# One-core PEER decoder step: one-hots, gather rows, V products and the residual issued in another order around the U and V sweeps

## The reference, cut to what matters

```python
def _layer(x, ...):
    h = _rmsnorm(x, norm1_g)
    ...
    merged = jax.nn.sigmoid(zga) * a_out + jax.nn.sigmoid(zgb) * b_out
    x = x + merged @ w_mix_out
    x = x + _peer(_rmsnorm(x, norm2_g), peer_wq, peer_k1, peer_k2, peer_u, peer_v)

def _peer(...):           # e: expert indices (tokens, 128), g: their softmax weights
    act = jax.nn.gelu(jnp.einsum('tkd,td->tk', u_tab[eb], hb))
    return jnp.einsum('tk,tkd->td', gb * act, v_tab[eb])

y_prompt = _rmsnorm(xp, final_g)
```

## Time and profile before

| | us |
|---|---|
| median of 3 runs (4887.19 to 4899.76) | 4889.77 |
| profiled execution, its time | 4888.54 |
| its span, first to last instruction | 4886.8 |
| PE busy | 4675.6 |
| DVE busy | 2655.6 |

### The profile page before, as it was taken

The page is one execution under the profiler, slowest core; times in us unless marked ns, Lnnn a source line. Parts: engine busy times, 40 slices in busy tenths (PEclk is TensorE's granted clock), DMA queues, the critical chain, the costliest instruction groups (busy, mean ns, idle before and its releaser), DMA issues.

```text
span 4886.8 us, 47196 instructions
## 1 busy us (share of the span) xinstructions
PE 4675.6 (96%) x18798; PEld 3394.6 (69%) x18798; DVE 2655.6 (54%) x4623; ACT 535.2 (11%) x1220; POOL 892.9 (18%) x691
## 2 busy tenths in 40 slices
PE   8999999999999999899999999999999989999995
PEld 7888888888756566566667678888888734444442
DVE  3433300018658576635555467775777755545555
ACT  1111200001111101110000111111222200000000
POOL 1000000000111212003333231112333222222222
PEclk9999999999999999999999999999999999999997
DMA  4334334553776758548889788778899899999997
GB/s 162 145 137 144 143 144 167 193 188 123 242 269 221 296 204 315 200 168 354 346 340 358 273 334 317 269 279 293 329 335 333 312 393 414 413 373 417 417 417 292
DMA packets 237853, 1352.17 MB, mean 277 GB/s; under 512 B 43185, under 2 KB 43441, under 8 KB 131138
## 3 DMA queue, kind: packets, MB, share of 16 engines
q1 hardware_dynamic: 143778, 665.97, 37.0%
q0 software_dynamic: 93856, 683.19, 36.0%
HBM read 1308.38 MB, written 40.16 MB: 276 GB/s over the span
## 4 chain that ended last, share of the span: by engine, by line
PE 56%; DMA 23%; DVE 14%; issue 4%; ACT 1%; POOL 1%; POOLq 0%; SPq 0%; DVEq 0%; ACTq 0%
PE ps L357 30%; PE ps L632 11%; DMA RING<-in_peer_v,table 7%; DMA RING<-in_peer_u,table 7%; PE ps L553 5%; DVE CUR L836 4%; DMA RING<-in_peer_v,X 4%; DVE RING L830 4%; DMA RING<-in_peer_u,X 4%; PE ps L495 3%; DVE BIG L1102 2%; PE ps L559 1%; PE ps L373 1%; DMA out<-BIG 1%; PE pm L402 1%
## 5 line engine op out<-in xcount | busy, mean ns | idle before, releaser
L357 PE MATMUL ps<-X,BIG 128*128 128x320 f32 (+1 forms) x5632 | 1400.1, 410 | 7.1 <-DVE BIG L1200 6.5
L357 PEld LDWEIGHTS ps<-X,BIG 128*128 128x128 f32 x5632 | 1070.8, 191 | 320.1 <-issue 18.1
L836 DVE SCALAR_TENSOR_TENSOR CUR<-RING,wexp,CUR 128x2048 f32<-128x2048 f32 x320 | 752.1, 2350 | 397.5 <-DMA RING<-in_peer_v,table 292.4
L830 DVE CUSTOM_DVE_ANT_0 RING<-RING,CUR 128x2048 f32<-128x2048 f32 x320 | 729.7, 2289 | 413.9 <-DMA RING<-in_peer_u,table 278.5
L632 PE MATMUL ps<-X,RA 128*128 128x256 f32 x4096 | 902.9, 381 | 5.4 <-DMA RA<-in_uT 4.0
L632 PEld LDWEIGHTS ps<-X,RA 128*128 128x128 f32 x4096 | 777.3, 191 | 112.2 <-DMA RA<-in_uT 4.3
L1800 POOL DMA_INDIRECT RING<-in_peer_u,table x256 | 364.9, 1426 | 1335.4 <-DVE hidden L830 991.5
L1800 POOL DMA_INDIRECT RING<-in_peer_v,table x256 | 363.0, 1418 | 1132.9 <-DVE CUR L836 814.4
L655 PE MATMUL ps<-RA,BIG 128*128 128x512 f32 x1024 | 489.7, 601 | 23.0 <-DMA RA<-in_peer_v 14.8
L655 PE MATMUL pm<-RA,BIG 128*128 128x512 f32 x1024 | 481.6, 592 | 0.0
L655 PEld LDWEIGHTS ps<-RA,BIG 128*128 128x128 f32 x1024 | 191.5, 191 | 279.4 <-issue 200.7
(11 more groups left out here) (291 smaller groups left out, 2923.8 us busy)
## 6 DMA issues: line engine op xcount, KB each, us to landing
BIG<-in_w_in_b SPq DMA_DIRECT2D x64, 2048.0 KB, 8.9
RA<-in_uT SPq DMA_DIRECT2D x256, 512.0 KB, 5.5
RA<-in_peer_v SPq DMA_DIRECT2D x256, 512.0 KB, 9.4
BIG<-in_w_gb_b SPq DMA_DIRECT2D x16, 2048.0 KB, 8.4
BIG<-in_w_ga_b SPq DMA_DIRECT2D x16, 2048.0 KB, 8.2
BIG<-in_w_gla_o_b SPq DMA_DIRECT2D x16, 2048.0 KB, 10.1
BIG<-in_w_mix_b SPq DMA_DIRECT2D x16, 2048.0 KB, 9.8
BIG<-in_w_q_b SPq DMA_DIRECT2D x16, 2048.0 KB, 9.3
```

Of the source, the lines that this page charges most:

```text
L357: last = pe.matmul(bank[:, 0:n], w[:, k, j * P:(j + 1) * P], src[:, k, 0:n], start=(k == 0), stop=(k == kt - 1))
L830: row_used.on(dve.tensor_tensor_reduce(out=row, in0=row, in1=h2cur[0:n, :], scale=1.0, scalar=0.0, op0=ALU.mult, op1=ALU.add, accum_out=hi ...
L836: row_used.on(dve.scalar_tensor_tensor(out=cur[0:n, :], in0=row, scalar=wexp[0:n, par, k:k + 1], in1=cur[0:n, :], op0=ALU.mult, op1=ALU.ad ...
```

## The change

- `G_AT` becomes 63, so the last gate product comes in U block 126 and block 127 has none. In a gated block DVE now runs `gate_tokens` of the block before, then the argument, then the one-hots of the next block, then H, and the rows last (budget 4.5 instead of 4.2). Before block 62 the budgets are 3.9 for routing and 2.8 for rows (3.6 and 2.0 before).
- Rows at more places: one at each of three points of `new_sample_states` in each head of group 1, budgets 14.4 and 9.6 in the first step of `gates(1)`.
- The change of tile: the gain is loaded into `h2cur` as soon as the last U row of a tile is used; the sum of squares goes to the ring; U rows of the next tile wait only for `query_in` (the load of `h2cur`), V rows for `cur_loaded`. The gather of the third row of a tile waits for the squares of the tile before.
- V by tile at its ends: block 0 multiplies tile 1 (in `pm`) for both halves ahead of tile 0, and the last two blocks do all of tile 0 ahead of tile 1.
- The residual comes back in 8 pieces of 256 KB and the gain in 4, one behind every eighth load of V from load 48 on.
- The end runs by tile, with squares in 4 pieces, the output in halves.

```diff
-G_AT = NB - PT // 4
+G_AT = NB - PT // 4 - 1
...
             pe.wait_ge(*gm_ready.at(PT // 4 - 1))
-            for b in range(NB):
+            for half in range(2):
+                v_product(0, half, 1)
+            pe.wait_ge(*h_ready.at(NB - 1))
+            for half in range(2):
+                v_half.on(v_product(0, half, 0), 0, half)
+            for b in range(1, NB - 2):
                 for half in range(2):
...
+                    v_product(b, half, 0)
+                    v_half.on(v_product(b, half, 1), b, half)
+            for t in range(2):
+                for b in range(NB - 2, NB):
+                    for half in range(2):
+                        last = v_product(b, half, t)
+                ps_done.on(last, "tile", t)
...
                     if b:
                         sample_state(h, b - 1)
+                    if b in (2, 4, 6):
+                        run(work, 2.4)
...
             def gates(g):
+                if g:
+                    spare((0, "gates1"), 14.4)
                 center(g)
                 finish(g, HEADS - 1)
+                if g:
+                    spare((0, "gates2"), 9.6)
                 layer_norm(g)
...
                 bank = banks.of("u", b)
+                if b > G_AT:
+                    gate_tokens(b - 1 - G_AT, b)
                 dve.wait_ge(*sq_u.at(b))
...
-                if b > G_AT:
-                    gate_tokens(b - 1 - G_AT, b)
                 spare((b, "u"), 0.0)
-                if b < G_AT:
-                    paced(work_1, 3.6)
-                paced(work, 2.0 if b < G_AT else 4.2)
+                if b < G_AT - 1:
+                    paced(work_1, 3.9)
+                    paced(work, 2.8)
+                elif b < NB - 2:
+                    onehots(b + 1 - G_AT)
...
-                if G_AT - 1 <= b < NB - 1:
-                    onehots(b + 1 - G_AT)
-            gate_tokens(PT // 4 - 1, NB)
+                if b >= G_AT - 1:
+                    paced(work, 4.5)
...
             def cur_load(t):
...
+                query_in.dma(pool.dma_start(h2cur[0:n, :], h2_d[t, 0:n, :]), t)
+                if t:
+                    yg_stored.dma(pool.dma_start(o[0][0, (t - 1) * P:t * P, :], cur[:, :]), t - 1)
+                    pool.wait_ge(*yg_stored.at(t - 1))
...
+            def gain_load(t):
+                pool.wait_ge(*row_used.at(last_u[t]))
+                fg_cur.dma(pool.dma_start(h2cur, a["final_g"].rearrange("(o d) -> o d", o=1).partition_broadcast(P)), t)
...
+                if m % ROWS == 2 and t:
+                    pool.wait_ge(*ss_g.at(t - 1))
...
-                if m == 2 * NB + 24:
-                    for t in range(2):
-                        x2_back.dma(sp.dma_start(x2b[:, t, :], x2_d[2 + t]), *((t,) if t == 0 else ()))
...
+                i = (m - 2 * NB - 48) // 8
+                cols = slice(512 * (i % 4), 512 * (i % 4) + 512)
+                if (m - 2 * NB) % 8 == 0 and 0 <= i < 8:
+                    x2_back.dma(sp.dma_start(x2b[:, i // 4, cols], x2_d[2 + i // 4, :, cols]), *((i,) if i < 7 else ()))
+                elif (m - 2 * NB) % 8 == 0 and 8 <= i < 12:
+                    fg_loaded.dma(sp.dma_start(final_g[:, cols], a["final_g"].rearrange("(o d) -> o d", o=1)[
+                        :, cols].partition_broadcast(P)), *((i,) if i < 11 else ()))
```

More of the change, by code:

```diff
@@ L645, in _, with v_product @@
                     ps_done.on(last, "g", q)
-            pe.wait_ge(*gm_ready.at(PT // 4 - 1))
-            for b in range(NB):
-                for half in range(2):
-                    m = 2 * NB + 2 * b + half
-                    pe.wait_ge(uv_loaded[slot_of[m]].sem, loads_of[m])
-                    for t in range(2):
[L653 to L657, removed]
+            def v_product(b, half, t):
+                m = 2 * NB + 2 * b + half
+                pe.wait_ge(uv_loaded[slot_of[m]].sem, loads_of[m])
+                for q in range(2):
+                    last = pe.matmul((ps, pm)[t][:, 2 * half + q, :], H[:, b, t * P:(t + 1) * P],
+                                     vhalf[slot_of[m]][:, q * 512:(q + 1) * 512], start=(b == 0), stop=(b == NB - 1))
+                return last
+            pe.wait_ge(*gm_ready.at(PT // 4 - 1))
+            for half in range(2):
[4 more added lines that the diff above has]
+            for b in range(1, NB - 2):
+                for half in range(2):
+                    v_product(b, half, 0)
[5 more added lines that the diff above has]
+                ps_done.on(last, "tile", t)
         @block.vector
@@ L853, in gather_rows @@
                             dve.wait_ge(*halves_met.at())
-                            step(dve.tensor_tensor(cur[0:NS, :], cur[0:NS, :], h2cur[0:NS, :], ALU.add))
-                        step(dve.tensor_tensor_reduce(out=h2cur[0:n, :], in0=cur[0:n, :], in1=cur[0:n, :], scale=1.0,
+                            step(dve.tensor_tensor(cur[0:NS, :], cur[0:NS, :], ring[0:NS, (m - 3) % 3, :], ALU.add))
+                        step(dve.tensor_tensor_reduce(out=ring[0:n, (m - 1) % 3, :], in0=cur[0:n, :],
+                                                      in1=cur[0:n, :], scale=1.0,
                                                       scalar=0.0, op0=ALU.mult, op1=ALU.add,
@@ L1297, in gate_tokens @@
                 dve.wait_ge(*ps_done.at("g", q))
[L1298 to L1299 removed]
+                dve.wait_ge(*g_copied.at(q))
                 dve.wait_ge(*h_ready.at(n - 1))
@@ L1349, in _ @@
                                  t, q)
-            for t in range(2):
-                dve.wait_ge(*ss3_done.at(t))
-                ms3_ready.on(dve.tensor_scalar(small[:, 14 + t:15 + t], small[:, 12 + t:13 + t], 1.0 / D, EPS, ALU.mult,
+                dve.wait_ge(*ss3_done.at(t, 3))
+                step(dve.tensor_reduce(small[:, 20 + t:21 + t], small[:, 12 + 4 * t:16 + 4 * t], AX.X, ALU.add))
+                ms3_ready.on(dve.tensor_scalar(small[:, 20 + t:21 + t], small[:, 20 + t:21 + t], 1.0 / D, EPS, ALU.mult,
                                                ALU.add), t)
-            dve.wait_ge(*fg_loaded.at())
-            for t in range(2):
                 dve.wait_ge(*root3.at(t))
-                step(dve.reciprocal(small[:, 16 + t:17 + t], small[:, 14 + t:15 + t]))
-                y_ready.on(dve.scalar_tensor_tensor(out=x2b[:, t, :], in0=x2b[:, t, :], scalar=small[:, 16 + t:17 + t],
-                                                    in1=final_g, op0=ALU.mult, op1=ALU.mult), t)
+                step(dve.reciprocal(small[:, 22 + t:23 + t], small[:, 20 + t:21 + t]))
+                for half in range(2):
+                    cols = slice(1024 * half, 1024 * half + 1024)
+                    y_ready.on(dve.scalar_tensor_tensor(out=x2b[:, t, cols], in0=x2b[:, t, cols],
+                                                        scalar=small[:, 22 + t:23 + t], in1=final_g[:, cols],
+                                                        op0=ALU.mult, op1=ALU.mult), t, half)
         @block.scalar
@@ L1716, in _ @@
                 serve(("end", i))
-            act.wait_ge(*fg_loaded.at())
+            act.wait_ge(*v_half.at(NB - 3, 1))
             for t in range(2):
[L1719 to L1723, removed]
+                for q in range(4):
+                    cols = slice(512 * q, 512 * q + 512)
+                    act.wait_ge(*sum_ready.at(t, q))
+                    ss3_done.on(fn(junk[:, t, cols], x2b[:, t, cols], ACT.Square,
+                                   accum_out=small[:, 12 + 4 * t + q:13 + 4 * t + q]), t, q)
                 act.wait_ge(*ms3_ready.at(t))
-                root3.on(fn(small[:, 14 + t:15 + t], small[:, 14 + t:15 + t], ACT.Sqrt), t)
+                root3.on(fn(small[:, 20 + t:21 + t], small[:, 20 + t:21 + t], ACT.Sqrt), t)
         @block.gpsimd
@@ L1802, in gather @@
                     bass.IndirectOffsetOnAxis(ap=idx, axis=0), bounds_check=NEXP - 1, oob_is_err=True), m)
+            last_u = [TOPK * max(i for i, unit in enumerate(units) if unit[0] == t and unit[2] == "u") + TOPK - 1
+                      for t in range(3)]
             cur_load(0)
```

63 lines of the change are left out of this document (32 added, 31 removed).

## The result

| | before | after |
|---|---|---|
| median, us | 4897.22 (4879.05 to 4914.12, 20 runs) | 4869.08 (4853.22 to 4884.82, 20 runs) |
| profiled execution, its time | 4888.54 | 4884.4 |
| its span | 4886.8 | 4882.7 |

The ratio is 0.9943, with a 95% interval of 0.9931 to 0.9956. The change gives 0.6% where 1.9% was forecast, and the time lies above the whole range (4764 to 4830). So the two profiles show 4.1 us between them where the medians show 28.1. I account for the span of the profiled execution first, and say at the end where its excess lies.

A forecast was written before the change was run, and what follows sets the result against it. The gather chain ended last, 27 us behind PE, the bound beneath. PE's end 4826.2+4+1+0-30-4.7-13.5 = 4783.0, plus 11.5 gave a span of 4794.5 and, with 1.74 and 1.2 added, 4797 us; 80% range 4764 to 4830.

The forecast's parts named there:

- Part 5: More rows in the sample section, gates(1) and ungated U blocks: +4 (0 to +24), +1 (0 to +6), 0 (-2 to +10) us.
- Part 4: V sweep, 906.1 us before: cut residual and gain loads shorten PE's waits, -13.5 us, bounds -20 and +5.
- a slack of 0.8 us: V sweep: fitted with 200 GB/s to the two old waits, subtracted from each piece's 1.3 us, leaving 0.5.
- Rival D: Residual and gain pieces in the V sweep pay a fixed cost each, +18 us: 4815; chance 0.07.
- The stall on load 4 of V: V sweep: allowance for load 4 arriving late, taking the sum from -15.3 to -13.5 us.
- Part 2: Gated U blocks: PE's wait for one-hots goes, 8.67 to 8.2 us a block, -30 us (bounds -54 and -1).
- My slot cycle: Gated U blocks: the second row waits for the slot the block before used first; 8.2 us a block on average.
- a sign of being wrong: Forecast is wrong if gated blocks take over 8.7 us, or if PE waits for U loads.
- rivals C and F: Gated U blocks. C: new wait replaces the old, 4826 us, chance 0.2. F: U loads bind, 4936 us, chance 0.03.
- Part 3: U to V: the 9.2 us between u(127) and V falls to 4.5, -4.7 us (0 to -8).
- Part 1: V sweep: 180 rows left instead of 226; the gather ends some 145 us ahead of PE and leaves the end.
- Part 6: The end: 11.5 us (9.5 to 14) from PE's last matmul to the end of the span.

The follow-up runs named there:

- The run with DVE's time alone: Changed kernel with an unused DVE reduction of a row's length replacing the row at three points of new_sample_states, so no gather starts: 4832.9 us, ratio 0.988.

## Why the prediction was wrong

- **Part 5, the sample sections: the step that failed.** I had +4 with bounds 0 and +24; it is +57 in the profiled execution. In the six profiled kernels that share all code up to the U sweep, the first U product starts at 2966.5, 2961.0, 2956.8, 2954.2, 2950.9 and 2948.8, so +47 is typical. The kernel before and the one with one-hots first, which share theirs, have 2909.3 and 2920.1, so that some 42 us are left between the two means, as by the medians (41.6). Of the 15.3 us by which the profiled execution exceeds its median, some 10 lie here, and 5 in its U sweep (986.3 us, where the eight profiled kernels with this code there have 981.5 on average). I named the right chain (store, then load, then PE), and priced it by DVE's 2.3 us. The run with DVE's time alone shows that this costs nothing. The price is that of a gather of 1 MB set off by the row, which lengthens each store and load of the chain, and, on top, PE's lower clock behind each wait. I had put 2 us of clock behind each V wait, and none here; the 12 us that I expected for in_state_gla are 30.4. My own question, what a faster engine triggers and what that collides with, would have led here: the earlier trace rows show room on DVE, and say nothing of SP's chain. Gates(1) at +1 is within what was seen.
- **Part 4, V sweep: wrong in sign (+13.9 for -13.5).** The step is "a piece of 256 KB costs 1.3 - 0.8 = 0.5 us". The first two waits behind pieces come 30.2 us apart in after, where eight loads take PE 27.5:

```profile
4135.65 1.98 PE L651 MATMUL ps<-RA,BIG 128*128 128x512 f32 x4 [0.82 <-DMA RA<-in_peer_v]
...
4165.81 1.98 PE L651 MATMUL ps<-RA,BIG 128*128 128x512 f32 x4 [1.68 <-DMA RA<-in_peer_v]
```

  That is 2.7 us for this piece. Over all twelve waits, the last at 4458.30, it is (4458.30 - 4135.65) / 11 = 29.3 us, so 1.8 us a piece, and the run that moves them gives 25 us for the twelve (920 - 895), 2.1 each, where I had 0.5. I had taken a slack of 0.8 us off each piece. My reading is that under the gather the V loads do not win it back between pieces, so that it can be spent once; no run shows that by itself. Without it my term would have been 12 x 1.3 = 16 us. Rival D pointed there, with a chance of 0.07, and would still have had the sweep at +4.5. The Trainium skill, "DMA: Bandwidth & Descriptors", section "Anatomy of one DMA", gives a fixed 2.0 us to each DMA on the path that POOL issues on (the pieces are SP's); the profiles have 1.3 for each further one, so less, yet far from my zero. The stall on load 4 of V came at 3975.04, but with 5.53 us and a slow group of 3.78 behind it, where I had allowed 1.8 in all and had said that no V wait would pass 2 us. These 5 to 6 us and the 21 that the pieces cost beyond my 4 are the miss of 27.4.
- **Part 2, gated blocks: the old wait rightly named, the new one not (8.41 for 8.2).** The wait for the one-hots is gone. By budgets 0, 3.6, 4.2 and 4.5 the blocks take 7.81, 7.90, 8.14 and 8.41 us; the seven other profiles at 4.5 have 8.25 to 8.42, and the mean of the eight is 8.35. My slot cycle, (7 x 8.6 + 5.4) / 8, gives 8.2 for the last; for 4.2 it gives (6 x 8.6 + 2 x 5.4) / 8 = 7.8. It runs 0.15 to 0.35 us low, and that it comes so near is in part luck. DVE does wait longer for rows, as I said it would, but PE never waits for DVE or ACT in these blocks. From 3410 to 3940 us it waits for U loads alone:

```profile
PE ps L632 <- DMA RA<-in_uT: 27.4, 25, 2.5
```

  That is 27.4 of the (8.41 - 7.81) x 63 = 38 us by which these blocks exceed PE's pace, and it is what I had named as a sign of being wrong: the transfer side of rivals C and F at a small size. The DMAs carry 353 GB/s here instead of 329:

```profile
3410.00:3940.00 530.00, 502.53 (x2526) 440.48 (x2525) 437.97 (x636) 143.66 (x446) 169.40 (x117) 0.99 0.93 353
```

  The gated part gives -17 us instead of -30. The ungated blocks gave about 6 us that I had not counted, and block 127, which now has no gate product and stands behind the last one, takes back 2.5.
- **Part 3, U to V: right.** 4.1 us for 4.5.
- **Part 1, fewer rows in V: right.** The gather leaves the end, and its last row is 167 us ahead of PE for the 145 I had. Three more rows (183) and a change of tile of 18.8 us instead of 13 made it later, not earlier; the margin is wider because V itself took 27 us longer than forecast. The gather had in fact more room than was needed, and that room was where the sample rows belonged: worked off in V they cost nothing that shows (V sweep 919 us against 920).
- **Part 6, the end: right.** 9.9 us for 11.5.

No rival had the loss in the heads, so the range (4764 to 4830) had no case for it. The parts that I had worked out from a stall in view (1, 3, 6, and the direction of 2) held. The two that failed were additions: the cover of the rows I had judged by DVE when SP's chain was the one at risk, and that of the pieces by a slack seen behind single large loads. Their bounds rested on these two readings, and so they were too narrow.

## What to carry to other kernels

An instruction that frees a buffer can cost what the transfer behind it does to the chains of small transfers around it, not its own time: look for a store that a load waits for and that PE waits for, and keep large gathers out of it. A short wait of PE is to be priced with the lower clock that follows. Once the gather no longer ends last, every row and every piece belongs where only spare DMA time is used. A slack found behind one large load is better not counted again for each piece.

## What the runs showed of the hardware that I had not expected

- Behind waits of only 4.44 and 2.74 us in a section whose groups are small, groups of four took 3.67 and 3.68 us instead of 1.93. Summed over 800 us this (0.05 of the granted clock, 40 us) cost more than the 22.5 us of waits.
- The same 256 KB cost 3.8 us as 32 partitions x 8 KB and 2.1 us as 128 x 2 KB, for the V loads queued behind it.
- With the gather over, 3 MB more on SP's queue brought PE no wait for V loads (V sweeps of 895 and 897 us; 917 to 920 with the same pieces under the gather).
